# Second input's product moved into the expert rounds, a ring of 22 places, and another route to the first round

## The chip, the cores and the metric

The kernel runs on one core of one Trainium2 chip. The metric is the device time of one execution in microseconds (us), median of three runs. Weights and inputs lie in HBM and come on chip by DMA; TensorE (PE) multiplies into PSUM, VectorE (DVE) and ScalarE (ACT) read PSUM and write SBUF, SyncE (SP) issues nearly all the transfers. Each engine runs its own program in order, and they meet at semaphores.

## The reference

The input is 256 tokens of 1024 features. Two layers of a first block (three attention-like branches and a convolved feed-forward part) are followed by two layers of a second block. The change is in the second block alone, in what follows its attention:

```python
x = layer_norm(ALPHA * x + mix, ln1_g[i], ln1_b[i])
ffn = hierarchical_moe(x, w_route_group[i], b_route_group[i], w_route_expert[i],
                       b_route_expert[i], w_exp_gate[i], w_exp_up[i], w_exp_down[i])
ple = jax.nn.sigmoid(x @ w_ple_gate[i]) * (p[i] @ w_ple[i])
x = layer_norm(ALPHA * x + ffn + ple, ln2_g[i], ln2_b[i])
```

`hierarchical_moe` chooses for each token one of 4 groups and in it the 2 best of 8 experts. There are 32 experts, each with three weight matrices of 1 MiB (gate, up, down). The second input `p` has 256 values a token; `w_ple` is 1 MiB and `w_ple_gate` 4 MiB.

## The kernel before

The second block of a layer runs its attention, then `wo` (four products `out_part(c, k, t)`, half c of the output columns, half k of the rows summed over, tile t of 128 tokens), the first layer norm (`norm_dve_of`, tile by tile on DVE with a square root on ACT), the routing, and then eight **rounds** of four experts each. In a round PE gathers 32 tokens an expert (`gather`, from `xg`, a copy of the normed x that ACT makes in `deal_features`), multiplies by the gate and up chunks (`hidden`, halves 0 and 1), turns, multiplies by the down chunks (`down`) and spreads the rows back (`give`). All 32 experts are always computed, so all 96 MiB of a layer's expert weights come in, and after round steps 1 and 4 the second gate is computed (`second_gate`, 32 matmuls of 512 columns, on 2 chunks of `w_ple_gate`).

**Chunks and the ring.** Every weight chunk of a round is 1 MiB. `expert_chunks` lists them in the order of use; a chunk goes to place j mod 20 of a ring of 20 places (`E_RING`), which lie over tiles that are done by then, and one chunk (`E_ONCE`) to a place that is used once. SP issues the first 21 loads one by one during `wo` and the routing, each as its place comes free (`first_loads(...)` in `sync`). After them `load_again` (L2200) issues each next load when the chunk 20 places earlier has been used. The last four down chunks come in halves (`load_last`, L2211), then the gains of the second layer norm, then the next layer's first chunks into the three `raw` tiles, each after the last expert chunk that lies there (`E_RAW`).

**From `wo` to the first round**, on PE: the eight `out_part`; `second_products(0)`, which is half of p @ w_ple (8 matmuls, L2943); the transposes of tile 0 of the normed x and its routing product (L2955); the same for tile 1; `second_products(1)`; the rank products (L2970 to L2972); the first gather (L2273). DVE computes the choice of experts from the logits (`first_of`, `top_of`; L3205, L3427 to L3461). ACT copies the turned x (`nT`), the two halves of the product (`pl`) and `xg`. `w_ple` has a tile of its own over `dqT`. Each of the last two first loads waits for `pl1`, since they go to `dqT` and to a tile that holds the turned p.

The order on every engine is written out by hand; PSUM halves are handed from user to user in the order of a list (`order`, `expert_lots`).

## Time and profile before

| | us |
|---|---|
| median of 3 runs | 1737.8 |
| lowest and highest | 1737.01, 1740.19 |
| the profiled execution, its own time | 1735.67 |
| its span | 1733.8 |
| PE busy | 1615.5 (93%) |
| DVE busy | 1070.4 (62%) |
| ACT busy | 756.2 (44%) |
| chain that ended last, PE / DMA / DVE | 72% / 12% / 8% |
| bytes moved | 422.82 MB, 244 GB/s in the mean |

The shares are means over stages that have different limits. In the span's slices DMA moves 110 to 200 GB/s for most of the time, and 410 to 418 GB/s in two stretches, about 1065 to 1250 us and 1515 to 1700 us: these are the rounds of the two layers of the second block. The change touches both, and the 80 us ahead of each.

### The profile page before, as it was taken

The page shows a single profiled execution, that of the slowest core. Times are in us where ns is not written, and L with a number is a line of the kernel's source. Part 1 is how long each engine was busy: PE and PEld are TensorE (multiplying, and loading weights), DVE is VectorE, ACT ScalarE, POOL GpSimd, SP SyncE. Part 2 cuts the span into 40 slices and gives each one's busy share as a digit, 9 for nine tenths or more (in the row PEclk, how much of TensorE's full clock was granted, in tenths as well). Part 3 has the DMA queues.
Part 4 walks back from the last instruction along what each step waited for, and adds up shares of the span by engine and source line. Part 5 has one row for each costly group of instructions (what it writes and reads, how often), then busy time and mean ns, then how long its engine had stood idle before and what let it go on. Part 6 is the DMA issues. An engine that isn't in the chain of part 4 may idle for free.

```text
span 1733.8 us, 26050 instructions
## 1 busy us (share of the span) xinstructions
PE 1615.5 (93%) x10632; PEld 1273.2 (73%) x10632; DVE 1070.4 (62%) x1506; ACT 756.2 (44%) x1006; POOL 0.2 (0%) x4
## 2 busy tenths in 40 slices
PE   7999999999999999999999999968779999898775
PEld 7877799998887789999887776534458777654433
DVE  5977768787786858777578762222165887422124
ACT  4556555545546645545455732101034566211111
POOL 0000000000000000000000000000000000000000
PEclk9999999999999999999999999989889999999888
DMA  7543445555553345554656498999965547999996
GB/s 251 175 168 116 164 166 179 189 191 173 189 188 110 127 164 191 187 194 152 210 178 207 147 415 329 416 418 412 411 225 195 201 146 289 362 414 415 413 415 263
DMA packets 174416, 422.82 MB, mean 244 GB/s; under 512 B 16000, under 2 KB 68584, under 8 KB 157672
## 3 DMA queue, kind: packets, MB, share of 16 engines
q1 hardware_dynamic: 174312, 421.33, 66.3%
q8 instruction: 77, 1.26, 0.3%
q14 instruction: 27, 0.22, 0.0%
HBM read 420.25 MB, written 1.05 MB: 243 GB/s over the span
## 4 chain that ended last, share of the span: by engine, by line
PE 72%; DMA 12%; DVE 8%; ACT 3%; SPq 2%; issue 2%; DVEq 0%; ACTq 0%
PE lot L289 18%; PE lot L291 17%; PE lot L290 17%; PE lot L2303 5%; DMA e_lo<-w_exp_up 4%; DMA two_e_sqT<-w_exp_up 3%; DVE w_lo L259 3%; PE lot L2377 2%; PE lot L2273 2%; PE lot L2330 2%; PE lot L416 2%; DMA two_e_dqT<-w_exp_up 2%; DMA two_prq<-w_exp_down 1%; PE lot L485 1%; DMA raw<-w_exp_down 1%
## 5 line engine op out<-in xcount | busy, mean ns | idle before, releaser
L259 DVE TENSOR_TENSOR w_lo<-raw,w_hi 128x2048 fp32r<-128x2048 f32 (+4 forms) x194 | 431.4, 2230 | 103.7 <-ACT w_hi L254 103.0
L254 ACT ACTIVATE w_hi<-raw 128x2048 fp32r<-128x2048 f32 (+4 forms) x194 | 361.2, 1867 | 122.8 <-PE lot L291 116.1
L289 PE MATMUL lot<-one_hT_hi,w_hi 128*128 128x256 f32 x704 | 199.3, 283 | 0.9 <-issue 0.9
L290 PE MATMUL lot<-one_hT_lo,w_hi 128*128 128x256 f32 x704 | 199.2, 283 | 0.0
L291 PE MATMUL lot<-one_hT_hi,w_lo 128*128 128x256 f32 x704 | 199.2, 283 | 0.0
L289 PE MATMUL lot<-w_hi,two_hT_hi 128*128 128x512 f32 (+1 forms) x448 | 176.9, 395 | 6.4 <-DVE two_hT_lo L382 3.1
L291 PE MATMUL lot<-w_hi,two_hT_lo 128*128 128x512 f32 (+1 forms) x448 | 172.5, 385 | 0.0
L290 PE MATMUL lot<-w_lo,two_hT_hi 128*128 128x512 f32 (+1 forms) x448 | 172.3, 385 | 0.0
L289 PE MATMUL lot<-w_hi,one_hT_hi 128*128 128x512 f32 (+2 forms) x384 | 148.7, 387 | 3.0 <-DVE w_lo L259 2.3
L291 PE MATMUL lot<-w_hi,one_hT_lo 128*128 128x512 f32 (+2 forms) x384 | 145.1, 378 | 0.0
L290 PE MATMUL lot<-w_lo,one_hT_hi 128*128 128x512 f32 (+2 forms) x384 | 145.0, 378 | 0.0
L289 PEld LDWEIGHTS lot<-one_hT_hi,w_hi 128*128 128x128 f32 x704 | 135.1, 192 | 2.0 <-issue 1.3
L290 PEld LDWEIGHTS lot<-one_hT_lo,w_hi 128*128 128x128 f32 x704 | 135.1, 192 | 0.7
L291 PEld LDWEIGHTS lot<-one_hT_hi,w_lo 128*128 128x128 f32 x704 | 135.1, 192 | 0.0
L289 PEld LDWEIGHTS lot<-w_hi,two_hT_hi 128*128 128x128 f32 x448 | 85.6, 191 | 26.3 <-issue 8.3
L1803 DVE SCALAR_TENSOR_TENSOR one_conv<-lot,one_cols,one_conv 128x255 f32<-128x255 f32 x160 | 66.2, 476 | 58.2 <-ACT one_conv L1488 55.7
L291 PEld LDWEIGHTS lot<-w_hi,two_hT_lo 128*128 128x128 f32 x448 | 85.5, 191 | 17.0
L290 PEld LDWEIGHTS lot<-w_lo,two_hT_hi 128*128 128x128 f32 x448 | 85.7, 191 | 14.9
L289 PEld LDWEIGHTS lot<-w_hi,one_hT_hi 128*128 128x128 f32 x384 | 72.2, 188 | 20.6 <-DVE w_lo L259 5.5
L291 PEld LDWEIGHTS lot<-w_hi,one_hT_lo 128*128 128x128 f32 x384 | 72.2, 188 | 13.0
L290 PEld LDWEIGHTS lot<-w_lo,one_hT_hi 128*128 128x128 f32 x384 | 72.3, 188 | 11.5
L2428 DVE COPY two_xw<-lot 128x512 f32<-128x512 f32 x16 | 11.1, 692 | 110.9 <-PE lot L2273 110.9
(457 smaller groups left out, 3235.6 us busy)
## 6 DMA issues: line engine op xcount, KB each, us to landing
raw<-w_in SPq DMA_DIRECT2D x78, 1024.0 KB, 5.1
raw<-ffn_w_up SPq DMA_DIRECT2D x44, 1024.0 KB, 5.1
raw<-ffn_w_down SPq DMA_DIRECT2D x22, 1024.0 KB, 5.0
raw<-w_out SPq DMA_DIRECT2D x16, 1024.0 KB, 6.2
e_lo<-w_exp_up SPq DMA_DIRECT2D x12, 1024.0 KB, 19.7
raw<-w_exp_down SPq DMA_DIRECT2D x12, 1024.0 KB, 17.4
e_hi<-w_exp_gate SPq DMA_DIRECT2D x10, 1024.0 KB, 19.1
e_hi<-w_exp_up SPq DMA_DIRECT2D x10, 1024.0 KB, 20.3
```

What stands on the lines that cost most here:

```text
L254: act.activation(K.hi[:, r, 0:n], self.raw(name)[:, 0:n], ACT.Copy).then_inc(K.sig["hi_ready"], 1)
L259: dve.tensor_tensor(K.lo[:, r, 0:n], self.raw(name)[:, 0:n], K.hi[:, r, 0:n].bitcast(F32), ALU.subtract).then_inc(K.sig["lo_ready"], 1)
L289: pe.matmul(out, a[0], b[0], start=start, stop=False)
L290: pe.matmul(out, a[0], b[1], start=False, stop=False)
L291: return pe.matmul(out, a[1], b[0], start=False, stop=stop)
L416: last = pe.matmul(s[:, h, t, 0:n], self.q(u, h)[:, t * P:(t + 1) * P], self.k(u, h)[:, 0:n], start=True, stop=True)
L485: last = pe.matmul(self.K.ps[3][h * HD:(h + 1) * HD, 0, q0:S], self.v(u, h, c), pt[:, h, c, q0:S], start=c == 0, stop=c == T - 1)
L1803: last = dve.scalar_tensor_tensor(dst, src, w, dst, ALU.mult, ALU.add)
L2273: last = pe.matmul(K.ps[1][:, lot - 2, kk * QE * CAP:(kk + 1) * QE * CAP], M.xg[:, t, k, :], M.rows01[:, t, :], start=t == 0, stop=t == T - 1)
L2303: last = pe.matmul(K.ps[0][j * CAP:(j + 1) * CAP, lot, half * D_E:(half + 1) * D_E], M.xw[:, k, rows], w[j][:, k, :], start=k == 0, stop=k ...
L2330: last = pe.matmul(K.ps[2][j * CAP:(j + 1) * CAP, n, :], M.h[:, f, j * CAP:(j + 1) * CAP], w[j][:, f, n * 512:(n + 1) * 512], start=f == 0 ...
L2377: last = pe.matmul(K.ps[1][:, lot - 2, :], M.nT[:, k, t * P:(t + 1) * P], w[:, k % 4, :], start=k == 0, stop=k == KD - 1)
```

## The change

The ring gets 22 places. `yT` and `hT_hi` (the turned x, `nT`) become places, `dqT` and the shared tile move forward in it, and the place used once now takes chunk 18. SP issues 23 loads ahead of the rounds, the last one when the routing product is filled.

The product p @ w_ple leaves the stretch before the rounds. Its weights come as two chunks of 512 KiB (`l0`, `l1`) just ahead of the gate's chunks, and go into a ring place whose other half takes the result. Since `nT` is a ring place now, the second gate turns x again from `xg` in the round (`second_turn`, 16 transposes each time, ACT copies them to the ring place of `n0` or `n1`, for which nothing is loaded); `w_ple_gate` is read in another order of rows to match.

On the way to the first round `out_part(1, 0, 1)` is moved back behind `out_part(1, 1, 0)`, so that tile 0 is complete earlier. The first layer norm gives its two halves of columns one after the other, and the transposes, copies and routing products follow half by half. Transposes of the identity are put between (6, 8, 12 and 4 of them). The choice of experts is rewritten with the top-8 instruction and its replacement over all 32 experts of a token, in place of the chain on 8 values. Some semaphores get other names, which are shared with the first block.

```diff
-E_RING = 20
-E_ONCE = 15
+E_RING = 22
+E_ONCE = 18
 PLE_AT = {0: 1, 1: 4}
 E_LOTS = 7
 LAST_TURNS = 44
-E_RAW = (10, 6, 9)
-E_SPLIT = ((15, 16), (11, 12), (13, 14))
-E_LN2 = 19
+E_RAW = (12, 8, 11)
+E_SPLIT = ((18, 19), (14, 15), (16, 17))
+E_LN2 = 20
+ROUTE_TURNS = (6, 8, 12, 4)
...
-            [K.raw[:, 2, :], K.raw[:, 0, :]] + \
-            [t[:, r, :] for r in (1, 2, 0) for t in (K.plain_hi, K.plain_lo)] + [t[:, :] for t in (e_prv, e_dqT, shared)]
+            [t[:, :] for t in (e_p, e_sqT, e_pt, e_yT, e_dqT)] + [K.raw[:, 1, :]] + \
+            [self.gates[:, t, :] for t in range(T)] + [K.raw[:, 2, :], K.raw[:, 0, :], shared[:, :]] + \
+            [t[:, r, :] for r in (1, 2, 0) for t in (K.plain_hi, K.plain_lo)] + [e_prv[:, :], e_nT[:, :]]
...
-            names += [f"pg{c}{k}" for c in range(2) for k in range(2) if PLE_AT.get(c) == q]
+            for c in range(2):
+                names += [f"n{c}", f"l{c}", f"pg{c}0", f"pg{c}1"] if PLE_AT.get(c) == q else []
...
+        if name[0] != "n":
+            self.wait_out(sp, self.held_before(name))
+            self.load(sp, name, self.expert(name))
...
+    def second_turn(self, pe, c, j):
+
+        name = f"N{c}.{j}"
+        lot = self.claim(pe, name)
+        for k in range(4):
+            last = pe.transpose(self.K.ps[1][:, lot - 2, k * P:(k + 1) * P], self.M.xg[:, j // 2, 4 * (j % 2) + k, :],
+                                self.K.ident[:, :])
+        last.then_inc(self.L.filled(name), 1)
+
+    def second_turned(self, act, c, j):
+
+        if j == 0:
+            self.wait_out(act, self.held_before(f"n{c}"))
+        lot = self.filled(act, f"N{c}.{j}")
+        act.activation(self.features(c)[:, 4 * (j % 2):4 * (j % 2) + 4, (j // 2) * P:(j // 2 + 1) * P],
+                       self.K.ps[1][:, lot - 2, :].rearrange("p (k s) -> p k s", k=4), ACT.Copy)\
+           .then_inc(self.L.drained(f"N{c}.{j}"), 1)
...
+        elif name[0] == "l":
+            eng.wait_ge(self.K.sig["e_placed"], int(name[1]) + 1)
...
+    def second_products(self, pe, c, t):
+
+        K, M = self.K, self.M
+        name = f"L{c}.{t}"
+        lot = self.claim(pe, name)
+        w = self.weights(pe, f"l{c}")
+        for k in range(2):
+            last = pe.matmul(K.ps[1][:, lot - 2, :], M.pT[:, k, t * P:(t + 1) * P], w[:, k, :], start=k == 0, stop=k == 1)
+        last.then_inc(self.L.filled(name), 1)
+
+    def second_taken(self, act, c, t):
+
+        lot = self.filled(act, f"L{c}.{t}")
+        act.activation(self.second(c, t), self.K.ps[1][:, lot - 2, :], ACT.Copy).then_inc(self.L.drained(f"L{c}.{t}"), 1)
+
     def second_gate(self, pe, c, t):
 
         K, M = self.K, self.M
         name = f"P{c}.{t}"
+        if t == 0:
+            for j in range(2 * T):
+                self.drained(pe, f"N{c}.{j}")
...
-            last = pe.matmul(K.ps[1][:, lot - 2, :], M.nT[:, k, t * P:(t + 1) * P], w[:, k % 4, :], start=k == 0,
+            last = pe.matmul(K.ps[1][:, lot - 2, :], self.features(c)[:, k, t * P:(t + 1) * P], w[:, k % 4, :], start=k == 0,
...
+        last.then_inc(self.K.sig["e_placed"], 1)
+        dve.wait_ge(self.K.sig["e_placed"], c + 1)
...
+    x = lambda h: K.x[:, t, h * 512:(h + 1) * 512]
+    centred = lambda h: dve.scalar_tensor_tensor(x(h), x(h), mean, g[:, h * 512:(h + 1) * 512], ALU.subtract, ALU.mult)
+    last = centred(0) if halves else [centred(h) for h in range(2)][-1]
     link(last)
     if between:
         between(dve)
     dve.wait_ge(K.sig[f"{tag}_root"], K.sig.at(f"{tag}_root", t + 1))
     link(dve.reciprocal(inv, K.stat[:, 2 + t:3 + t]))
     for h in range(2):
-        x = K.x[:, t, h * 512:(h + 1) * 512]
-        dve.scalar_tensor_tensor(x, x, inv, b[:, h * 512:(h + 1) * 512], ALU.mult, ALU.add)\
+        if halves and h:
+            link(centred(h))
+        dve.scalar_tensor_tensor(x(h), x(h), inv, b[:, h * 512:(h + 1) * 512], ALU.mult, ALU.add)\
            .then_inc(K.sig[f"{tag}_normed"], 1)
...
-              ("pT", 3), ("nTt0", 0), ("pl0", 3), ("pl1", 2), ("nTt1", 0), ("rt", 1), ("rank", 0), ("count", 0)]
+              ("pT", 3), ("nTt0", 0), ("nTt1", 3), ("rt", 1), ("rank", 0), ("count", 0)]
...
-            return A["w_ple_gate_2"][layer][k * 512:(k + 1) * 512, c * 512:(c + 1) * 512].rearrange("(k p) c -> p k c", p=P)
+            return A["w_ple_gate_2"][layer].rearrange("(p k) c -> p k c", p=P)[:, 4 * k:4 * k + 4, c * 512:(c + 1) * 512]
...
                 first_loads(5)
+                L.wait_filled(sp, "bd1")
+                first_loads(6)
             if name == "wo11":
                 L.wait_filled(sp, "bs1")
-                sp.dma_start(M.w_ple[:, :, :], A["w_ple_2"][layer].rearrange("(k p) c -> p k c", p=P))\
-                  .then_inc(sig["wple_in"], 16)
+                first_loads(7)
         sp.wait_ge(sig["lo_ready"], ST.ready["wo10"])
-        first_loads(6)
+        first_loads(8)
         sp.wait_ge(sig["merged"], sig.at("merged", 4))
-        first_loads(7, 8)
+        first_loads(9, 10)
         sp.wait_ge(sig["lo_ready"], ST.ready["wo01"])
-        first_loads(9)
+        first_loads(11)
         sp.wait_ge(sig["lo_ready"], ST.ready["wo11"])
-        first_loads(10)
+        first_loads(12)
+        L.wait_filled(sp, "pT")
+        first_loads(13)
         ST.wait_used(sp, "wo10")
-        first_loads(11, 12)
+        first_loads(14, 15)
         ST.wait_used(sp, "wo01")
-        first_loads(13, 14)
+        first_loads(16, 17)
         ST.wait_used(sp, "wo11")
-        first_loads(15, 16, 17)
+        first_loads(18, 19, 20)
         sp.wait_ge(sig["n1_normed"], sig.at("n1_normed", 2 * T))
-        first_loads(18)
-        L.wait_filled(sp, "pl1")
-        first_loads(19, 20)
+        first_loads(21)
+        L.wait_filled(sp, "rt")
+        first_loads(22)
...
-        ST.done(out_part(1, 0, 1), "wo10")
         both("mT1")
         out_part(0, 1, 0)
         out_part(1, 1, 0).then_inc(L.filled("wot0"), 1)
+        ST.done(out_part(1, 0, 1), "wo10")
...
+        def turn_normed(t):
+
+            lot = L.claim(pe, f"nTt{t}")
+            dst = flat(K.ps[lot][:, :, :])
+            for k in range(KD):
+                if k % 4 == 0:
+                    pe.wait_ge(sig["n1_normed"], sig.at("n1_normed", 2 * t + k // 4 + 1))
+                last = pe.transpose(dst[:, k * P:(k + 1) * P], K.x[:, t, k * P:(k + 1) * P], K.ident[:, :])
+                if k == 3:
+                    last.then_inc(sig["half_ready"], 1)
+            last.then_inc(L.filled(f"nTt{t}"), 1)
 
         def route_tile(t):
 
@@ -2950,19 +3012,23 @@
             if t == 0:
                 L.claim(pe, "rt")
                 pe.wait_ge(sig["w_route"], sig.at("w_route", 32))
-            both(f"nTt{t}")
+            pe.wait_ge(sig["nT_copied"], sig.at("nT_copied", t + 1))
             for k in range(KD):
+                if k == 4:
+                    both(f"nTt{t}")
                 last = pe.matmul(K.ps[lot][:, t, 0:N_ROUTE], M.nT[:, k, t * P:(t + 1) * P], M.w_route[:, k, :],
                                  start=k == 0, stop=k == KD - 1)
             if t:
                 last.then_inc(L.filled("rt"), 1)
 
-        second_products(0)
-        transpose_tile(K, L, pe, K.x, "nTt0", 0, sig, "n1_normed")
+        turn_normed(0)
+        lot = L.claim(pe, "nTt1")
+        keep_awake(K, pe, lot, ROUTE_TURNS[0])
         route_tile(0)
-        transpose_tile(K, L, pe, K.x, "nTt1", 1, sig, "n1_normed")
+        keep_awake(K, pe, lot, ROUTE_TURNS[1])
+        turn_normed(1)
         route_tile(1)
-        second_products(1)
+        E.warm(pe, ROUTE_TURNS[2])
...
+            lot = L.use[f"nTt{t}"][0]
+            quarter = lambda b: (M.nT[:, 4 * b:4 * b + 4, t * P:(t + 1) * P],
+                                 K.ps[lot][:, b, :].rearrange("p (k s) -> p k s", k=4))
+            act.wait_ge(sig["half_ready"], sig.at("half_ready", t + 1))
+            act.activation(*quarter(0), ACT.Copy).then_inc(sig["nT_copied"], 1)
+            L.wait_filled(act, f"nTt{t}")
+            act.activation(*quarter(1), ACT.Copy).then_inc(L.drained(f"nTt{t}"), 1)
...
-        take("pl1", M.pl[:, 1, :, :], whole)
...
+        link(dve.tensor_reduce(st[:, 140:142], g, AX_X, ALU.max))
+        top = st[:, 140:142].unsqueeze(2).to_broadcast([P, T, N_G])
+        link(tt(small, g, top, ALU.is_equal))
+        tt(M.r[:, 0, :, 0:N_G], g, top, ALU.subtract).then_inc(sig["group_shift"], 1)
+        link(dve.scalar_tensor_tensor(small, small, -100.0, M.iota[:, 0:N_G].unsqueeze(1).to_broadcast([P, T, N_G]),
+                                      ALU.mult, ALU.add))
+        link(dve.tensor_reduce(st[:, 146:148], small, AX_X, ALU.min))
+        link(tt(cold, small, st[:, 146:148].unsqueeze(2).to_broadcast([P, T, N_G]), ALU.is_gt))
+        for t in range(T):
+            last = dve.scalar_tensor_tensor(by_group(M.r32[:, t, :]), cold[:, t, :].unsqueeze(2).to_broadcast([P, N_G, E_G]),
+                                            NEG, by_group(e[:, t, :]), ALU.mult, ALU.add)
+        link(last)
+        for t in range(T):
+            last = dve.max(M.top8[:, t, :], M.r32[:, t, :])
+        link(last)
+        link(dve.memset(M.top8[:, :, 2:8], PICKED))
+        for t in range(T):
+            last = dve.match_replace(M.w32[:, t, :], M.top8[:, t, :], M.r32[:, t, :], PICKED)
+        link(last)
+        dve.tensor_scalar(M.r32_r[:, :, :], M.w32[:, :, :], -2e38, None, ALU.is_lt).then_inc(sig["selected"], 1)
+        tt(M.r32[:, :, :], M.r32[:, :, :], M.top8[:, :, 0:1].to_broadcast([P, T, N_E]), ALU.subtract)\
+            .then_inc(sig["expert_shift"], 1)
```

PE in layer 0 of the second block, from the end of `wo` to the first gather. Before:

```order
L2943 MATMUL lot<-two_w_ple,two_pT 128x512 x4
L886 MATMUL lot<-ident,x 128x128 x8
L2955 MATMUL lot<-two_w_route,two_nT 128x36 x8
L886 MATMUL lot<-ident,x 128x128 x8
L2955 MATMUL lot<-two_w_route,two_nT 128x36 x8
L2943 MATMUL lot<-two_w_ple,two_pT 128x512 x4
L2970 MATMUL lot<-two_r_153,two_tri_r 128x32
L2971 MATMUL lot<-two_r_153,two_tri_r 128x32
L2972 MATMUL lot<-two_r_153,two_tri_r 128x32
L2273 MATMUL lot<-two_rows_143,two_xg 128x128 x16
```

The same place now:

```order
L3004 MATMUL lot<-ident,x 128x128 x8
L894 MATMUL lot<-ident 128x128 x6
L3019 MATMUL lot<-two_w_route,two_nT 128x36 x8
L894 MATMUL lot<-ident 128x128 x8
L3004 MATMUL lot<-ident,x 128x128 x8
L3019 MATMUL lot<-two_w_route,two_nT 128x36 x8
L2402 MATMUL lot<-ident 128x128 x12
L3036 MATMUL lot<-two_r_152,two_tri_r 128x32
L3037 MATMUL lot<-two_r_152,two_tri_r 128x32
L3038 MATMUL lot<-two_r_152,two_tri_r 128x32
L2402 MATMUL lot<-ident 128x128 x4
L2308 MATMUL lot<-two_rows_142,two_xg 128x128 x16
```

Both products on `w_ple` have gone from here (a row's count is that of the instructions written; the trace shows each of these fp32 matmuls as two).

SP in layer 0, from the load of the last `wo` chunk to the eleventh load behind it, before:

```order
L2655 DMA raw<-w_out 128x4x512
L2696 DMA two_w_ple<-w_ple 128x2x1024
L2200 DMA raw<-w_exp_up 128x2048
L2200 DMA two_gates<-w_exp_up 128x2048
L2200 DMA two_gates<-w_exp_gate 128x2048
L2200 DMA raw<-w_exp_gate 128x2048 x2
L2200 DMA e_hi<-w_exp_gate 128x2048
L2200 DMA e_lo<-w_exp_up 128x2048
```

Now, from one load further ahead:

```order
L2211 DMA two_e_yT<-w_exp_up 128x2048
L2713 DMA raw<-w_out 128x4x512
L2211 DMA two_e_dqT<-w_exp_up 128x2048
L2211 DMA raw<-w_exp_gate 128x2048
L2211 DMA two_gates<-w_exp_gate 128x2048 x2
L2211 DMA raw<-w_exp_gate 128x2048
L2211 DMA raw<-w_exp_up 128x2048
L2211 DMA two_e_shared<-w_exp_up 128x2048
```

A load into `yT` stands ahead of the last `wo` chunk, and an expert chunk stands where `w_ple` stood.

PE at the second gate of round step 1, before:

```order
L2273 MATMUL lot<-two_rows_143,two_xg 128x128 x16
L2285 MATMUL lot<-ident,two_wrows 128x128 x2
L2377 MATMUL lot<-two_gates,two_nT 128x512 x16
L2330 MATMUL lot<-raw,two_h 32x512 x2
L2330 MATMUL lot<-e_hi,two_h 32x512
```

Now:

```order
L2308 MATMUL lot<-two_rows_142,two_xg 128x128 x16
L2320 MATMUL lot<-ident,two_wrows 128x128 x2
L2228 MATMUL lot<-ident,two_xg 128x128 x16
L2411 MATMUL lot<-two_e_yT,two_pT 128x512 x4
L2430 MATMUL lot<-two_e_dqT,two_e_pt 128x512 x4
L2430 MATMUL lot<-raw,two_e_pt 128x512 x4
```

The transposes of x and half of p @ w_ple stand ahead of the gate, which now reads its features from a ring place.

## Rows read from the trace of the kernel before

**Rows 1.** Windows, layer 0: stretch, length, engines' busy time, PE clock, DMA share, GB/s.

```profile
1040.00:1045.00 5.00, 3.89 (x18) 3.84 (x18) 0.18 (x1) 4.28 (x3) 0.00 (x0) 0.50 1.03 411
1045.00:1050.00 5.00, 5.00 (x11) 2.06 (x10) 4.24 (x26) 0.59 (x3) 0.00 (x0) 0.73 0.19 78
1050.00:1055.00 5.00, 4.08 (x40) 3.82 (x43) 1.86 (x9) 2.74 (x3) 0.00 (x0) 1.00 0.87 301
1055.00:1060.00 5.00, 5.00 (x88) 2.92 (x84) 1.46 (x5) 0.00 (x0) 0.00 (x0) 1.00 0.46 149
1060.00:1065.00 5.00, 5.00 (x72) 3.76 (x63) 1.54 (x5) 0.76 (x2) 0.00 (x0) 1.00 0.96 403
...
1065.00:1250.00 185.00, 152.18 (x1420) 85.18 (x1419) 44.50 (x76) 23.41 (x35) 0.00 (x0) 0.93 1.02 415
```

**Rows 2.** Windows, layer 1, the same stretch.

```profile
1500.00:1505.00 5.00, 2.81 (x18) 1.96 (x17) 3.82 (x20) 1.02 (x1) 0.00 (x0) 1.00 0.92 329
1505.00:1510.00 5.00, 5.00 (x73) 3.82 (x75) 0.69 (x1) 1.88 (x2) 0.00 (x0) 1.00 0.54 224
1510.00:1515.00 5.00, 5.00 (x87) 2.68 (x76) 1.97 (x7) 0.00 (x0) 0.00 (x0) 1.00 0.62 210
...
1515.00:1700.00 185.00, 155.90 (x1433) 88.32 (x1430) 43.82 (x76) 24.15 (x36) 0.00 (x0) 0.93 1.02 415
```

**Rows 3.** Timeline of SP's queue: start, duration, line, transfer; both layers.

```profile
1049.83 0.37 SPq L2200 DMA_DIRECT2D two_e_dqT<-w_exp_down  x1
1050.24 0.47 SPq L2200 DMA_DIRECT2D two_e_shared<-w_exp_gate  x1
1058.41 0.34 SPq L2200 DMA_DIRECT2D two_e_spare<-w_exp_gate  x1
...
1510.89 0.34 SPq L2200 DMA_DIRECT2D two_e_spare<-w_exp_gate  x1
```

**Rows 4.** Timeline of PE, layer 0, from the end of `wo` to the first gather.

```profile
1030.33 3.59 PE L2943 MATMUL lot<-two_w_ple,two_pT 128*128 128x512 f32 x8
...
1033.76 1.04 PE L886 MATMUL lot<-ident,x 128*128 128x128 f32 x8
...
1044.59 5.20 PE L2943 MATMUL lot<-two_w_ple,two_pT 128*128 128x512 f32 x8
...
1051.00 3.81 PE L2273 MATMUL lot<-two_rows,two_xg 128*128 128x128 f32 x32 [0.92 <-issue]
```

**Rows 5.** Timeline of DVE: layer norm and routing of layer 0, routing of layer 1.

```profile
1036.24 1.42 DVE L2579 SCALAR_TENSOR_TENSOR x<-x,stat,two_ln_b 128x512 f32<-128x512 f32 x2
...
1044.82 0.23 DVE L3205 TENSOR_TENSOR two_logit<-lot,two_route_b 128x72 f32<-128x72 f32 x1 [7.16 <-PE lot L2955]
...
1049.08 0.43 DVE L3205 TENSOR_TENSOR two_r<-two_r 128x16 f32<-128x16 f32 x2
...
1497.31 0.23 DVE L3205 TENSOR_TENSOR two_logit<-lot,two_route_b 128x72 f32<-128x72 f32 x1 [4.31 <-PE lot L2955]
```

**Rows 6.** DVE groups by form: what the top-8 instructions take on 128 values.

```profile
L3287 DVE MAX8 two_top<-two_work 128x8 f32<-128x128 f32 x16 | 4.7, 291 | 0.3
L3291 DVE MATCH_REPLACE8 two_work<-two_top,two_work 128x128 f32<-128x128 f32 x16 | 4.4, 276 | 0.0
```

**Rows 7.** Chain that ended last, rounds of layer 0: start, duration, what.

```profile
1095.45 13.74 PE lot L2377 x32
...
1119.56 25.44 DMA e_lo<-w_exp_up
```

**Rows 8.** End of layer 0: ACT, then DVE, then landing of the next layer's first chunk.

```profile
1267.09 0.68 ACT L254 ACTIVATE w_hi<-raw 128x576 fp32r<-128x576 f32 x1 [0.20 <-DMA raw<-w_in]
...
1272.54 0.16 DVE L2576 RECIPROCAL stat<-stat 128x1 f32<-128x1 f32 x1
...
raw<-w_in SPq DMA_DIRECT2D x1, 288.0 KB, 10.4
...
raw<-w_in SPq DMA_DIRECT2D x1, 288.0 KB, 3.0
```

191 lines of the change are left out of this document (79 added, 112 removed).

## The prediction

> **What bounds the kernel now.** I read the page's slices first, then windows over the rounds, then SP's queue, then PE and DVE between `wo` and the first gather. PE is busy for 93% of the span, but not in the rounds, and the change touches only these and the stretch ahead of them. In the rounds of layer 0 DMA moves 415 GB/s for 185 us on end with a busy share of 1.02, while PE is busy for 152.2 of the 185 us [rows 1]; in layer 1 it is 415 GB/s and 155.9 us [rows 2]. The chain walks there through the landing of a chunk, 25.44 us after its issue [rows 7], so some ten chunks are in flight. The rounds end when their bytes are in. At 415 GB/s a chunk of 1.049 MB costs 2.53 us. The reader should look for the one thing that moves such an end: time in which DMA stands still after it has become full. There is one such hole in each layer. In layer 0 the windows from 1045 to 1065 us show 78, 301, 149 and 403 GB/s [rows 1]. Against 415 that is 20 us less (931/415) x 5 us = 20 - 11.22 = **8.78 us** of lost transfer. In layer 1 three windows show 329, 224 and 210 [rows 2]: 15 - (763/415) x 5 = **5.81 us**.
>
> Why the hole is there: the first 21 loads have been issued, and the next may go only when the first chunk has been used, at 1058.41 us in layer 0 and 1510.89 us in layer 1 [rows 3]. Also the last two first loads went late, at 1049.83 and 1050.24 us [rows 3], since they waited for `pl1`.
>
> **More loads ahead of the rounds.** The total of bytes stays: `w_ple` (1 MiB) leaves the stretch ahead and comes back as two halves, `n0` and `n1` load nothing. Ahead of the first reload stand two loads more and `w_ple` less, so one chunk net, 2.53 us of cover. In layer 0, with about 2 us from the reload's issue to its first bytes (a small transfer of 288 KB landed in 3.0 us on an idle queue [rows 8], of which 0.7 are bytes), the old set was done at 1060.4 - 8.78 = 1051.6 us of transfer time; the new one would be at 1054.2. In layer 1 it is 1512.9 - 5.81 + 2.53 = 1509.6. To leave no hole the first chunk must be used by 1052.2 and 1507.6, which is 6.2 and 3.3 us earlier than now. The new first loads must themselves come in time: counting chunks, the changed list is at every wait level with the old or ahead of it until `wo` is done (`yT` is free early), and the last two, behind the norm and the routing product, are issued by about 1039 us.
>
> **An earlier first gather.** On PE the first eight matmuls of the product take 3.59 us between `wo` and the transposes [rows 4]; they go. DVE finishes the norm of tile 1 at 1036.24 + 1.42 = 1037.66 [rows 5]. With tile 0 filled one `out_part` earlier, DVE is free when tile 1 is filled at about 1030.4. Two operations of half a tile's columns at the rate of L2579 (0.7 us each), the second statistics (0.7), the mean and root (some 0.5) and the centring and scaling (4 x 0.7) put the end at about 1035.6. Transposing 4 of 8 (1.04 us for 8 [rows 4]), a half copy (0.6), and half the routing product (about 1 us) follow, the first halves being done already: logits at about 1038.4 against 1044.82 [rows 5], **6.4 us** earlier. In layer 1, where the clock did not fall, the same steps give 1493.8 against 1497.31 [rows 5], **3.5 us**. The `xg` copies on ACT (2 us each) end before the gather needs them.
>
> **The choice of experts.** From the logits to the end of the selection it is 1049.51 - 1044.82 = 4.69 us now [rows 5]. The new chain has some 14 dependent steps. The top-8 instructions take 291 and 276 ns on 128 values [rows 6]; on 32 I take about 0.2 us, as for the other small DVE operations. The bounds are 0.15 and 0.29 us for each of the four, 0.3 us either way. The sum is about 2.85 us: **1.8 us** less. The second half of the product, 5.20 us of PE beside the old chain [rows 4], is gone too; in layer 0 it ended at 1049.79, no earlier than the selection, so the rank products would otherwise not have profited. Rank, rows and gather keep their 1.5 us. Together the first gather, at 1051.00 now [rows 4], comes 8.2 us earlier in layer 0 and 5.3 us earlier in layer 1. Both are 2.0 us more than is needed. So both holes close: -8.8 and -5.8 us.
>
> **Turns of the identity.** In layer 0 the clock stood at 0.50 of 2.4 GHz from 1040 to 1045 us and was mixed to 1050 [rows 1], after PE had waited for copies; in the same stretch of layer 1 the window shows 1.00 [rows 2]. The 30 transposes fill waits. If they fail, routing product and transposes run at the level of before, 1.2 GHz, and cost up to 2 us more, which is the margin just worked out. Bounds 0 and +2 us; I take 0.
>
> **The second gate in the rounds.** It gains 16 transposes (2.1 us, at 1.04 for 8) and half of the product (3.59 us), with waits for ACT's copies about 7 us in all, beside the 13.74 us that it takes [rows 4, 7], twice in a layer. PE was idle for 32.8 and 29.1 us of each 185 [rows 1, 2], so 14 us fit, and the 10 chunks in flight keep DMA going. Cost 0; uncovered, 14 us a layer. The waits on `e_placed` stand at the end of DVE's step of the gate; behind them are only DVE's adds, on an engine with 44.5 of 185 us busy [rows 1]. The ring place of `n` and the one of `l` are held during a gate of some 21 us, in which 8 chunks land; with `n`, `l` and the two gate chunks held, 18 of the 22 places are left for them.
>
> **Half-size transfers.** The last eight loads of a layer are of 512 KiB already and the stream stays full over them up to 1250 us [rows 1], so the two new ones cost 0 in the sum. The Trainium skill (DMA: Bandwidth & Descriptors, Bandwidth) gives 341 GB/s for a lone 1 MB transfer and 425 for 16 MB and advises at least 1 MiB; halves at, say, 290 GB/s would by that rule add about 0.5 us each, 2 us in all (an estimate from that page). This trace does not agree where the queue is full: 415 GB/s with single chunks of 1 MiB.
>
> **The end of layer 0.** The next layer's first chunk now goes over the place of the last down chunk but two, which is free only when the last matmul is done (about 1266.1 us on the old scale). Before, it landed at 1267.09, 10.4 us after its issue, behind the stream; on an idle queue the like of it took 3.0 us [rows 8]. It would land at about 1269.5. ACT then needs 0.7 + 1.3 + 0.2 + 0.2 us, and its root is wanted by 1272.54 us [rows 8], so it just fits. Bounds: 0 and, with a landing as slow as before, 10.4 - 3.7 = +6.7 us. I take 0, being nearer to the idle row, since nothing else is in the queue.
>
> **Sum.** Against the profiled execution (1735.67 us): -8.8 - 5.8 = -14.6, giving 1721.1. That execution lies 2.1 us under the median of 1737.8; on the median's scale the forecast is **1723.2 us**.
>
> **Rivals.**
> A. *The holes close in part.* The clock falls in the routing all the same, or the half-by-half steps hide less than I count. With 4 us less advance a layer the holes keep 2 us each: -10.6, 1727.2 us. For it: the layers differ by 3 us there now. Against: 2 us of margin in both.
> B. *The hand-over at the end of layer 0 waits for the raw chunk* behind the last matmul, up to +6.7: about 1729.9 us. For it: the sum for ACT is tight. Against: the idle landing.
> C. *The gate starves DMA.* `n`, `l` and two gate chunks are held at once, and DMA pauses for a third of the 14 us of added work, 4.5 us a layer: -14.6 + 9, about 1732 us.
> D. *Nothing moves*, because the stream's rate, not its holes, absorbs the gain (the rate sinks when the first loads come closer): 1737.8 us. Against: full windows on both sides of the hole show the same 415.
> E. *Slower: PE becomes the bound of the rounds.* PE's work in the 185 us of layer 0 becomes 152.2 + 14 = 166 us, of 185 - 8.8 = 176. It is the bound when the granted clock of the rounds falls from 0.93 [rows 1] below 0.93 x 166 / 176 = 0.88, and the gain is lost when PE needs 7.3 us over the 176, at 0.84. At 0.82 it is 188 us, 12 us over, in each layer: 1737.8 - 14.6 + 24 = 1747 us. For it: PE does wait between chunks, and its clock is already mixed. Against: the share of waiting gets smaller.
>
> **How the numbers follow.** Forecast 0.66, A 0.12, B 0.07, C 0.06, D 0.03, E 0.06. The forecast's own range is 1720 to 1726; below it I leave 1718, since timed runs whose clock falls in layer 1 as well have a larger hole (5.8 could be 8.8, 3 us more to gain). Up to 1731 takes in A, B and some of C, so the range is 1718 to 1731, with about 0.15 outside. 0.2% is 3.5 us, about what a measurement of this kernel can tell from no change. Faster by more: forecast, A, B, C, 0.91. Within: D, 0.03. Slower: E, 0.06.
>
> **What would show it.** Right: windows of 5 us show about 415 GB/s with no dip from 1000 us to the end of layer 0's rounds, and in layer 1; 22 loads before the first reload, which is issued near 1050 us; the first gather near 1043 us; the clock at 1.00 in the routing; the gate some 21 us with DMA full. Wrong: a dip that stays, a dip behind the gates, an ACT wait of over 2 us for `raw` at the end of layer 0, or a mean rate in the rounds below 410 GB/s.

## Result and the profile after

Before: 1738.49 us (median of 4 runs, 1737.01 to 1740.19). After: **1724.88 us** (4 runs, 1722.88 to 1727.42). The ratio is 0.9922 with a 95% interval of 0.9905 to 0.994, so 13.6 us less (10 to 17). The forecast was 1723.2 us, with a range of 1718 to 1731. One of the four executions of a kernel below (`halves_p`, 1991.41 us) ran in a slower state, and its ratio leaves that one out.

The profiled execution of after took 1727.42 us (span 1725.6), only 8.2 us less span than the 1733.8 of before. It is the slowest of its four, and the one of before was faster than every timed run beside it, so the two traces have to be compared by stretches. First the transfers: windows of after, layer 0, columns as in [rows 1].

```profile
1035.00:1040.00 5.00, 5.00 (x45) 4.83 (x44) 4.08 (x9) 3.30 (x4) 0.00 (x0) 1.00 1.03 424
1040.00:1045.00 5.00, 4.01 (x35) 3.54 (x33) 2.24 (x12) 4.18 (x4) 0.00 (x0) 1.00 1.01 406
1045.00:1050.00 5.00, 3.59 (x30) 3.38 (x31) 2.98 (x18) 1.25 (x4) 0.00 (x0) 1.00 1.02 408
1050.00:1055.00 5.00, 5.00 (x79) 3.28 (x77) 0.69 (x1) 1.36 (x2) 0.00 (x0) 1.00 1.03 424
1055.00:1060.00 5.00, 5.00 (x77) 3.23 (x77) 2.39 (x8) 0.38 (x1) 0.00 (x0) 1.00 1.01 418
1060.00:1065.00 5.00, 5.00 (x70) 4.02 (x72) 1.09 (x3) 0.60 (x1) 0.00 (x0) 1.00 1.01 421
1065.00:1250.00 185.00, 160.65 (x1458) 91.03 (x1454) 43.54 (x74) 30.36 (x46) 0.00 (x0) 0.95 1.02 413
```

The same in layer 1:

```profile
1495.00:1500.00 5.00, 4.70 (x52) 4.27 (x56) 2.22 (x8) 1.88 (x2) 0.00 (x0) 1.00 1.03 416
1500.00:1505.00 5.00, 5.00 (x90) 2.88 (x85) 1.55 (x7) 0.00 (x0) 0.00 (x0) 1.00 1.02 419
1505.00:1510.00 5.00, 5.00 (x64) 4.08 (x57) 0.90 (x2) 0.98 (x2) 0.00 (x0) 1.00 1.01 423
```

Where [rows 1, 2] had 78, 301, 149 and 329, 224, 210 GB/s, no window is below 406. Both holes are gone, and the clock of the routing in layer 0 is 1.00 (it was 0.50). Why they are gone stands in SP's queue (columns as in [rows 3]): the last two of the first loads, then the first reload, and the same of layer 1.

```profile
1040.68 0.53 SPq L2211 DMA_DIRECT2D two_e_prv<-w_exp_gate  x1
1043.16 0.33 SPq L2211 DMA_DIRECT2D two_e_nT<-w_exp_gate  x1
1054.83 0.33 SPq L2211 DMA_DIRECT2D two_e_spare<-w_exp_gate  x1
...
1491.04 0.33 SPq L2211 DMA_DIRECT2D two_e_nT<-w_exp_gate  x1
1502.71 0.33 SPq L2211 DMA_DIRECT2D two_e_spare<-w_exp_gate  x1
```

And on PE in layer 0, from the end of `wo` over the second tile's routing product and the ranks to the first gather:

```profile
1035.51 1.03 PE L3004 MATMUL lot<-ident,x 128*128 128x128 f32 x8
...
1041.20 1.93 PE L3019 MATMUL lot<-two_w_route,two_nT 128*128 128x36 f32 x16
...
1045.99 0.28 PE L3036 MATMUL lot<-two_r,two_tri_r 128*128 128x32 f32 x1 [1.52 <-DVE two_r L3521]
...
1047.42 3.81 PE L2308 MATMUL lot<-two_rows,two_xg 128*128 128x128 f32 x32 [0.42 <-issue]
```

DVE: the logits and the selection in layer 0, the logits in layer 1.

```profile
1043.17 0.23 DVE L3281 TENSOR_TENSOR two_logit<-lot,two_route_b 128x72 f32<-128x72 f32 x1 [2.52 <-PE lot L3019]
...
1045.74 0.20 DVE L3521 TENSOR_SCALAR two_r<-two_w 128x64 fp32r<-128x64 f32 x1
...
1491.05 0.23 DVE L3281 TENSOR_TENSOR two_logit<-lot,two_route_b 128x72 f32<-128x72 f32 x1 [2.52 <-PE lot L3019]
```

Everything ahead of the rounds lies 5.2 us later in this execution (1035.51 against 1030.33 [rows 4]), so steps are measured from the end of `wo`. The logits come 7.7 us behind it (before 14.5), the first gather 11.9 us (before 20.7), the first reload 19.3 us (before 28.1).

**Where the time went.** The two ends of layer 1's dense part in before are its first product and the end of `wo`:

```profile
1278.68 0.40 PE L289 MATMUL lot<-w_hi,two_hT_hi 128*128 128x72 f32 x1 [3.11 <-DVE two_hT_lo L382]
...
1485.66 3.59 PE L2943 MATMUL lot<-two_w_ple,two_pT 128*128 128x512 f32 x8
```

In after they are 1275.32 and 1483.39 us. That gives four parts:

- from the end of `wo` in layer 0 to layer 1's first product: 248.35 us before, 239.81 after, **-8.5**
- from the end of `wo` in layer 1 to the end: 248.1 before, 242.2 after, **-5.9**
- ahead of layer 0's routing, in code that the change doesn't touch: +5.2
- layer 1's dense part: 207.0 before, 208.1 after, +1.1

The first two sum to -14.4 and are the change. The third is chance: all of it is there by 910 us (the same load of `w_in` is issued at 904.93 us before and at 910.10 after), where both kernels still run the same code. Of its 5.2 us, 3.75 are there by 64 us: a load landed late, and PE's clock fell during the wait. The waits of PE for the first block's latents, before and after:

```profile
PE lot L1127 <- DVE one_lat L1580: 1.3, 1, 1.3
```

```profile
PE lot L1128 <- DVE one_lat L1581: 3.2, 1, 3.2
```

Ten of the kernels traced here share this code and that of the layers ahead, word for word; they issue the load of `two_e_nT` in layer 0 between 1037.73 and 1043.66 us, and after is at 1043.16. That puts the end of `wo` between 1030.1 and 1036.0 us; in the two traces with the old code (before, and `choice` below) it is at 1030.33 and 1032.55. The fourth part comes back below (the hand-over).

### The profile page after: what moved, and what is told of

Read it like the earlier page. It is cut to its first block, busy times and chain, and to the rows that moved or that the text cites. A ratio compares the mean times of both kernels' runs of the same rounds, so it can differ in the third digit from the quotient of the medians.

```text
span 1725.6 us, 26332 instructions
## 1 busy us (share of the span) xinstructions
PE 1623.5 (94%) x10756; PEld 1283.2 (74%) x10756; DVE 1067.8 (62%) x1494; ACT 767.6 (44%) x1030; POOL 0.2 (0%) x4
## 4 chain that ended last, share of the span: by engine, by line
PE 74%; DMA 10%; DVE 9%; ACT 3%; SPq 2%; issue 2%; DVEq 0%; ACTq 0%
PE lot L290 18%; PE lot L292 17%; PE lot L291 17%; PE lot L2338 5%; DMA two_gates<-w_exp_up 4%; DMA two_e_spare<-w_exp_up 3%; DVE w_lo L260 3%; PE lot L2430 3%; DMA two_e_prv<-w_exp_down 3%; PE lot L2308 2%; PE lot L2365 2%; PE lot L417 2%; PE lot L486 1%; ACT w_hi L255 1%; PE lot L476 1%
## 5 line engine op out<-in xcount | busy, mean ns | idle before, releaser
L292 PEld LDWEIGHTS lot<-w_hi,one_hT_lo 128*128 128x128 f32 x384 | 72.6, 189 | 13.1
```

Source lines behind the costliest of these rows:

```text
L292: return pe.matmul(out, a[1], b[0], start=False, stop=stop)
```

## Experiments

All are against the changed kernel, but for the last one. Ratios are to the kernel before on the same chip, whose medians there were 1738.42 (first four), 1739.32 (next four) and 1736.71 us (last four), so kernels of different groups are compared by their ratios: 0.001 is 1.7 us.

**How much earlier than needed the gather is.** Two kernels with turns of the identity ahead of the first gather. A turn is a transpose of the identity whose result nobody reads; it takes PE 0.114 us (44 of them took 5.03).

```diff
         both("rt")
+        E.warm(pe, 35)        # 105 in the second kernel
         E.gather(pe, 0)
```

> The changed kernel with 35 more turns of the identity on PE right ahead of the first gather of each layer: at 0.114 us a turn (44 turns took 5.03 us in the trace of after) 4.0 us of delay, of which about 0.6 us falls into PE's wait for the rows. My theory: after the change the stream has a margin. In the trace of after the last of the first loads is issued at 1043.16 us and lands 17.7 us later, at 1060.9, while the first reload is issued at 1054.83 and needs some 2 us to its first bytes, so about 4 us are to spare in each layer. The delay stays inside it: 1724.9 us, 0 to +1 us. Rival, the gather itself is on the path (PE's work in the rounds is the bound): +3.4 us in each layer, 1731.7 us.

> The same with 105 turns, 12.0 us, of which 11.4 count. My theory: beyond the margin of 4 us every us of delay opens a hole of one us in the transfers, (11.4 - 4) = 7.4 us in each layer, +15 us in all: about 1740 us, and windows of 5 us show the hole near 1060 us as in the kernel before. Rival, the gather on the path from the start: +23 us, 1748 us. Rival, the hole was not what set the time of before: no change, 1725 us.

Measured: 1725.55 us, ratio 0.9923 (0.9899 to 0.9947), and 1739.31 us, ratio 1.0004 (0.9991 to 1.0017). The second has given back the whole gain. Its windows in layer 0 and its first reload:

```profile
1050.00:1055.00 5.00, 5.00 (x48) 5.00 (x47) 0.00 (x0) 0.00 (x0) 0.00 (x0) 1.00 0.61 251
1055.00:1060.00 5.00, 5.00 (x59) 4.45 (x61) 0.69 (x1) 1.88 (x2) 0.00 (x0) 1.00 0.02 7
1060.00:1065.00 5.00, 5.00 (x89) 2.88 (x85) 1.76 (x7) 0.00 (x0) 0.00 (x0) 1.00 0.32 82
```

```profile
1040.02 0.33 SPq L2211 DMA_DIRECT2D two_e_nT<-w_exp_gate  x1
1062.50 0.33 SPq L2211 DMA_DIRECT2D two_e_spare<-w_exp_gate  x1
```

From `two_e_nT` to the first reload it is 11.67 us in after, 14.84 with 35 turns, 22.48 with 105: 3.2 and 10.8 us later. From `two_e_nT` to layer 1's first product it is 232.2, 233.8 and 241.0 us: 1.7 and 8.8 us longer. With 35 turns a small hole is open already (329 and 367 GB/s from 1055 to 1065 us). So the first 1.5 to 2.0 us are free, and from there each us costs about one. By the medians the cost of 105 turns is 14.3 us in two layers, which leaves 3.6 us free in each. The rule holds; how large the margin is stays open between 1.5 and 3.6 us. My 4 us was too large by the traces, and the prediction's 2.0 was nearer.

**Whether ring places and an earlier gather are one sum.** The 35 turns, and two places of cover less:

```diff
         sp.wait_ge(sig["n1_normed"], sig.at("n1_normed", 2 * T))
-        first_loads(21)
         L.wait_filled(sp, "rt")
-        first_loads(22)
+        E.wait_out(sp, E.names[0])
+        first_loads(21)
+        first_loads(22)
```

> The kernel with 35 turns ahead of the first gather, and the last two of the first loads held until the first chunk has been used: the cover of two ring places (5.06 us) is taken away. My theory: the cover and the earlier gather are one sum. The margin of 4 us becomes -1, and the delay of 3.4 us adds to it, so the hole is 3.4 + 5.06 - 4.1 = about 4.4 us in each layer, +8.7 us against the kernel with the turns alone: about 1734 us. If the ring places are worth nothing (only the gather counts), it is as fast as with the turns alone, 1725 us.

Measured: 1735.05 us, ratio 0.998 (0.9968 to 0.9991), 9.5 us over the kernel with the 35 turns alone, where 8.7 were expected. The windows from 1045 to 1060 us are at 360, 29 and 360 GB/s. Two places less are worth what 5 us of later gather are.

**The turns in the routing.**

```diff
-ROUTE_TURNS = (6, 8, 12, 4)
+ROUTE_TURNS = (0, 0, 0, 0)
```

> The changed kernel without the 30 turns of the identity in the routing. My theory: the granted clock falls to 0.50 in the routing of layer 0 as it did before the change, the gather comes up to 2 us later there, and the margin of 4 us takes that: 1724.9 us, 0 to +1. Rival, the turns are what makes the change work: the gather comes 4 us or more later in both layers and the hole comes back in part, +2 to +6 us, 1727 to 1731 us.

Measured: 1726.18 us, ratio 0.9929 (0.9905 to 0.9952). One window of layer 0, and one of layer 1:

```profile
1040.00:1045.00 5.00, 1.30 (x5) 1.22 (x6) 3.71 (x24) 1.59 (x3) 0.00 (x0) 0.50 1.02 409
```

```profile
1500.00:1505.00 5.00, 5.00 (x92) 2.90 (x84) 1.42 (x7) 0.00 (x0) 0.00 (x0) 1.00 0.69 234
```

The clock falls to 0.50 again, and now in layer 1 too (0.50 from 1485 to 1495 us, where before and after both show 1.00). The transfers do not stay full: 393 and 390 GB/s from 1050 to 1060 us, and the 234 shown in layer 1. From the end of `wo` the first reload takes 22.2 and 23.8 us, where after has 19.3 in both layers: 2.9 and 4.5 us more. The stretches behind the end of `wo` (to layer 1's first product, and to the end) take 241.1 and 244.7 us against 239.8 and 242.2: 1.3 and 2.5 us more. That is once more the delay less 1.5 to 2.0 us. The traces so put the price of leaving the turns out at 3.8 us, the medians at 1.3 (ratio +0.0007), which is within the spread. My expectation that the margin takes the delay is not what the windows show; they show the rival's picture, a hole that comes back in part, while the time is not told apart from no change.

**Room for PE in the rounds.** 5 and 15 us more ahead of each gate.

```diff
+                    E.warm(pe, 44)        # 132 in the second kernel
                     E.second_gate(pe, c, 0)
```

> The changed kernel with 44 more turns of the identity on PE (5.0 us) ahead of each of the two gates of a layer, 20 us of PE work in all. My theory: PE has room in the rounds (160.65 us busy of the 185 us from 1065 to 1250 in the trace of after), the gate grows from about 20 to 25 us, ten loads cover it, and the time stays: 1724.9 us, 0 to +1. Rival, the gate already stands at the edge of starving the transfers or PE is the bound: +5 us a gate, up to +20 us, 1745 us.

> The same with 132 turns, 15 us a gate, 60 us of PE work in all. My theory: now PE is the bound of the rounds: 160.65 + 30 = 190.7 us of work in 185 us, so at least +6 us a layer, +12 us, about 1737 us; up to +25 us if transfers stop while a gate of 35 us holds four chunks and uses none. Windows of 5 us then show dips of the transfers behind the gates. Rival, no limit near: 1725 us. Rival, each gate is on the path: +60 us, 1785 us.

Measured: 1724.99 us, ratio 0.9927 (0.9903 to 0.995), and 1744.87 us, ratio 1.0033 (1.0015 to 1.0051). 5 us a gate are free; with 15 it is 19 to 20 us slower than the changed kernel. Windows of layer 0 with 132 turns, the gate from 1091 to 1125 us:

```profile
1115.00:1120.00 5.00, 5.00 (x13) 2.21 (x12) 0.69 (x1) 0.58 (x1) 0.00 (x0) 1.00 1.04 420
1120.00:1125.00 5.00, 5.00 (x13) 2.09 (x11) 0.00 (x0) 0.00 (x0) 0.00 (x0) 1.00 0.59 247
1125.00:1130.00 5.00, 5.00 (x57) 1.85 (x60) 0.69 (x1) 1.48 (x2) 0.00 (x0) 1.00 0.59 210
1130.00:1135.00 5.00, 4.68 (x58) 2.61 (x46) 4.34 (x7) 1.80 (x3) 0.00 (x0) 1.00 0.31 75
```

SP issues no load from 1105.5 to 1125.4 us in this trace, and the transfers run dry some 17 us into that. This is rival C's mechanism, at a gate of 34 us; at 20 us (after) and 25 us (44 turns) it does not appear. PE's busy time is 176.06 of the 185 us from 1065 to 1250, so my first estimate, that PE's sum of work would be the bound there, is not what this shows: the dip comes first.

**What a transfer in halves costs.** Every reload but the last ones as two transfers, split along the rows.

```diff
-        sp.dma_start(self.chunk(name), self.source(name[0], expert)).then_inc(self.landed(name), 16)
+            for n in range(2):
+                sp.dma_start(dst[:, n * KD // 2:(n + 1) * KD // 2, :], src[:, n * KD // 2:(n + 1) * KD // 2, :])\
+                  .then_inc(self.landed(name), 16)        # down chunks: by halves of the columns
```

> The changed kernel with every reload of 1 MiB in the rounds but the last ones split into two transfers of 512 KiB, on the same queue one behind the other; some 37 chunks a layer. My theory: behind a full queue the size of a transfer from 1 MiB down to 512 KiB costs nothing: 1724.9 us, -1 to +1, with 413 GB/s in the rounds. Rival, the size rules the rate even in a full queue, at the half microsecond for each MiB in halves that the prediction named: 37 x 0.54 = 20 us a layer, 1765 us.

Measured: 1737.98 us, ratio 0.9999 (0.9986 to 1.0012): 13 us slower than whole transfers, so my theory fell. The count of 37 was wrong as well: SP issues 152 transfers in layer 0's rounds instead of 83, so 69 are split in a layer, and 13.1 / 138 is **0.10 us for each MiB**, not 0.54. The queue from 1065 to 1240 us, after and with halves (a gate or up chunk comes in packets of 8 KB, and with halves only 12 of 26488 packets are that long, where after has 5116 of 14940):

```profile
DMA packets 14940, 72.41 MB, mean 414 GB/s; under 512 B 1120, under 2 KB 1120, under 8 KB 9824
```

```profile
DMA packets 26488, 69.80 MB, mean 399 GB/s; under 512 B 2058, under 2 KB 2058, under 8 KB 26476
```

By the sources in the code, a gate or up chunk of a partition is one contiguous piece of 8 KB, a down chunk two of 4 KB, a chunk of the gate's weights four of 2 KB; halves are 4 KB and 2 KB. The rates of the windows follow: some 420 GB/s for 8 KB, 405 to 410 for 4 KB, 386 to 397 for 2 KB, and with halves they alternate between 410 and 388. Two kernels test whether it is the piece or the transfer that counts.

```diff
+            for n in range(2):
+                sp.dma_start(dst[n * 64:(n + 1) * 64], src[n * 64:(n + 1) * 64]).then_inc(self.landed(name), 16)
```

> The changed kernel with the same reloads split in two as before, but by partitions: 64 and 64, so that no contiguous piece gets shorter, while each transfer is again of 512 KiB. Splitting along the rows cost 13 us and took the rate in the rounds from 414 to 399 GB/s, with 26488 packets instead of 14940 in 175 us. Theory A, the length of the pieces set that: 1724.9 us, -1 to +1, and 414 GB/s. Theory B, the size of the transfer or the number of transfers set it: about 1738 us again.

Measured: 1923.56 us, ratio 1.1047 (1.1015 to 1.1078). Neither theory has this: transfers to 64 partitions have a price of their own, much larger than the one sought (281 GB/s, below). The Trainium skill (DMA: Bandwidth & Descriptors, Rules for kernel authors) advises against two transfers to disjoint halves of the partitions, since they serialize. This trace agrees with the advice, and it shows more than serializing would cost: 281 GB/s where whole transfers, one behind the other, had 415. This run doesn't separate A from B. The next one does, with transfers of the same size and longer pieces:

```diff
-        return rows.rearrange("(k p) c -> p k c", p=P) if kind == "D" else rows.rearrange("(p k) c -> p k c", p=P)
+        return rows.rearrange("(p k) c -> p k c", p=P)
...
-            last = pe.transpose(K.ps[3][:, 0, f * P:(f + 1) * P], M.act[:, 1, f * P:(f + 1) * P], K.ident[:, :])
+            last = pe.transpose(K.ps[3][:, 0, f * P:(f + 1) * P], M.act[:, 1, :].rearrange("s (p f) -> s f p", f=2)[:, f, :],
+                                K.ident[:, :])
```

> The kernel with both groups of hand-over turns, and in it w_exp_down read so that each partition's two rows lie side by side in memory (pieces of 8 KB instead of 4 KB; PE's transpose of the activations picks every second column to match). In the trace of after the windows of the rounds show about 420 GB/s where gate and up chunks are loaded (pieces of 8 KB) and 388 to 410 where down chunks are. My theory: the length of the piece sets the rate. 24 down chunks of 1 MiB a layer at about 403 GB/s take 2.60 us, at 420 GB/s 2.50: 2.4 us a layer, -5 us against the kernel with the turns alone, about 1714 us. Rival, the dips have another cause (loads beside ACT's and DVE's work, or the order on the queue): no change.

Measured: 1720.08 us, ratio 0.9893 (0.9873 to 0.9912), 3.6 us under the kernel it is built on (`hand2` below, 1723.69; 0.9898 to 0.9936), where 5 were expected. The two intervals overlap, so the gain in time is likely rather than certain; in the two traces the stretches behind the end of `wo` are 0.6 us (layer 0) and 2.6 us (layer 1) shorter. The rates are clearer. The window from 1090 to 1240 us of after, with halves, with longer pieces, and by halves of the partitions:

```profile
1090.00:1240.00 150.00, 127.35 (x1059) 69.58 (x1062) 36.10 (x62) 26.08 (x39) 0.00 (x0) 0.94 1.02 415
```

```profile
1090.00:1240.00 150.00, 123.65 (x1017) 65.93 (x1015) 34.10 (x58) 23.19 (x34) 0.00 (x0) 0.92 1.04 400
```

```profile
1090.00:1240.00 150.00, 129.77 (x1072) 71.11 (x1074) 36.08 (x62) 26.20 (x39) 0.00 (x0) 0.94 1.02 419
```

```profile
1090.00:1240.00 150.00, 92.58 (x694) 49.68 (x693) 23.06 (x41) 16.48 (x26) 0.00 (x0) 0.81 1.02 281
```

(`hand2` has 415 GB/s there, as after has.) With longer pieces most of the dips go to 415 to 424 GB/s, and what is left at 1070 to 1080, 1165 to 1175 and 1245 to 1255 us (385 to 406) are, by the order of the loads, the chunks of the gate's weights and the last halves, both of 2 KB pieces. So the piece sets the rate (together with the distance in memory between the pieces of a partition, which changes with it). Whether the number of transfers adds something was not separated; whole chunks of 4 KB pieces and halves of 4 KB pieces both ran at 405 to 410.

**The hand-over between the layers.** In after PE waits 5.27 us for DVE's norm behind the last product, then 2.64 us for the first operand. The clock, 0.82 from 1265 us, is at 0.50 from 1270, and it stays there until about 1285.2 us (the window from 1285 shows 0.98):

```profile
1280.00:1285.00 5.00, 5.00 (x18) 4.42 (x19) 1.23 (x1) 2.57 (x2) 0.00 (x0) 0.50 0.61 204
```

Two kernels:

```diff
         E.give_half(pe, NQ - 1, 1)
+        if before is None:
+            E.warm(pe, 40)                        # the first kernel asks `if out is None`, see below
...
         if ahead:
             keep_awake(K, pe, lot, INDEX_TURNS)
+        if before:
+            keep_awake(K, pe, lot, 18)
```

> The changed kernel with 40 turns of the identity behind the last product of layer 0 and 18 more between the transposes of the next layer's first tile and its first product. In the trace of after PE is idle for 5.3 and 2.6 us there, the granted clock falls to 0.50 until about 1285.2 us, and 9.9 us of work at half the clock cost 4.9 us, the eight transposes 0.9 more. My theory: with the turns the clock stays at 1.00 over the hand-over: -4 to -6 us against the changed kernel, about 1720 us. Rival, the clock falls all the same, or the turns stand in front of the transposes: 0 to +1 us, 1725 us.

> The kernel with the turns at the hand-over from layer 0 to layer 1, now with both groups: 40 turns behind the last product of layer 0 (the run before this one held only the 18 behind the transposes of the first tile, since a name in the code meant something else there; it came to 1719.4 us, and its granted clock rose at about 1270.6 us instead of 1285.2). My theory: with both the clock does not fall at all, the eight transposes of the first tile take 1.04 us instead of 1.94, and that is on the path: 0.9 us less, 1718.5 us. Rival, the 18 turns have all there is to gain: 1719.4 us.

In the first the condition on the 40 turns read a name that PE's part of the code uses for something else, so only the 18 turns ran. Measured: **1719.44 us, ratio 0.9895** (0.9876 to 0.9915), and with both groups 1723.69 us, ratio 0.9917 (0.9898 to 0.9936). The 18 turns alone take 5.4 us off the changed kernel (4.7 by the ratios), as expected of both groups; the 40 give 3.8 to 4.3 us of it back. PE with 18 turns:

```profile
1266.99 1.94 PE L887 MATMUL lot<-ident,x 128*128 128x128 f32 x8 [5.25 <-DVE x L2634]
1268.72 3.07 PE L894 MATMUL lot<-ident 128*128 128x128 f32 x18
1271.54 0.28 PE L290 MATMUL lot<-w_hi,two_hT_hi 128*128 128x72 f32 x1
```

And with both groups:

```profile
1265.77 4.53 PE L2402 MATMUL lot<-ident 128*128 128x128 f32 x40
1275.08 1.93 PE L887 MATMUL lot<-ident,x 128*128 128x128 f32 x8 [4.78 <-issue]
```

With 18 turns the products of layer 1 start at 0.28 us each (0.40 in after): the clock is back after the turns, some 4 us behind the end of PE's wait, not 14. With both groups the clock did not stay up as expected: the eight transposes take 1.93 us again. With the 40 turns PE waits 4.78 us and the profile shows no engine that it waits for. Behind these turns stands the conditional jump over the overflow rounds. In after the same 4.8 us could lie inside the wait for DVE, and the turns, queued ahead of the jump, would push it out from under that cover. That the jump is the cause is read from the place and the releaser "issue", and no run moves the jump alone.

The clock also accounts for the +1.1 us of the fourth part: PE is busy at half the clock for 9.9 us behind the hand-over in after (1275.3 to 1285.2), for 7.9 in before (1278.7 to 1286.6, with the window from 1285 at 0.84). 2 us more at half the clock cost 1.0 us. That the change is the reason is not shown. In seven more traces with the same code at this place the time at half the clock, counted up to the first 512-column product at full speed, runs from 7.6 us (no turns in the routing) and 8.2 (35 turns) to 9.8; by this count after has 9.9, and the two traces with the old code 8.1 each.

**The new choice of experts alone**, in the kernel before (DVE's chain from the logits to the weights as in the change, all else as before; the diff is that part of the change).

> The kernel before with one part of the change alone, the new choice of experts. The selection gets 1.9 us shorter (from the logits to the first gather 6.18 us before, 4.25 after, in layer 0). My theory: in layer 0 the second half of PE's product (at half the clock) ends at 1049.79 us, where the old selection ended at 1049.51, so the gather comes no earlier and the hole stays; in layer 1 the product ends at about 1500.8 us, and the hole there shrinks by 1.9 us: 1738.4 - 1.9 = 1736.5 us. Rival, both layers gain: 1734.6 us. Rival, the selection is not on the way to the first reload: 1738.4 us.

Measured: 1737.12 us, ratio 1.0002 (0.9989 to 1.0015). The interval of 4.5 us holds the -1.9 of the theory barely and rules the rival's -3.8 out. PE in layer 0 of this kernel:

```profile
1046.43 5.62 PE L2943 MATMUL lot<-two_w_ple,two_pT 128*128 128x512 f32 x8
1051.48 0.58 PE L2970 MATMUL lot<-two_r,two_tri_r 128*128 128x32 f32 x1
```

The ranks wait for nothing but PE's own product, as expected, and the windows from 1045 to 1065 us (275, 102, 318, 228 GB/s) hold a hole of 8.9 us, as before. In layer 1 it is (1245 - 876) / 415 x 5 = 4.4 us instead of 5.8. So no gain in time is shown for the selection alone, and in layer 0 the trace shows none in the hole. That it pays once the product has left its place is argued from these rows; no run has the rest of the change without it.

## Why the prediction was right, step by step

**The bound.** Transfers bound the rounds, and the holes were the only loss. Right: the change took -8.5 and -5.9 us where -8.8 and -5.8 were forecast, and opening a hole again by delay alone gave the whole gain back, at one us for one us.

**More loads ahead.** One chunk of net cover is 2.53 us. The run with two places less confirms the trade: 9.5 us for two layers, 8.7 by this sum. The sign of 22 loads ahead of the first reload was miscounted: SP issues 23 (numbers 0 to 22), as the change says, and the trace has the first reload as the 24th.

**An earlier gather.** Forecast 6.4 us for the logits in layer 0 and 3.5 in layer 1; measured from the end of `wo` 6.8 and 4.0 (in layer 1 11.65 to 7.66 us). First gather: forecast 8.2 and 5.3 earlier; measured 8.8 and 5.9. The half us is an addition in the prediction. From the norm's end at 1035.6 us its steps (0.5, 0.6 and 1) give logits at 1037.7, and it wrote 1038.4. On its scale the trace has the norm's end at 1035.5 and the logits at 1038.0. The margin of 2.0 us is 1.5 to 2.0 in the traces, 3.6 by the medians.

**The choice of experts.** Forecast 1.8 us; from the logits to the gather it is 6.18 us before and 4.25 after, 1.9. MAX8 and MATCH_REPLACE8 on 32 values took 0.29 us (two together, pipelined) and 0.17, inside the bounds.

**Turns of the identity.** Forecast 0 with a bound of +2. They did not fail: the clock is 1.00. But the price named for their failure was low. Without them the first reload comes 2.9 and 4.5 us later and the clock falls in layer 1 too, so the margin does not cover it: +3.8 us by the traces, +1.3 by the medians, inside the spread.

**The second gate.** Forecast a gate of about 21 us and no cost. It runs from 1091.7 to 1111.8 us, and nothing stops. The chain through it and behind:

```profile
1094.44 3.66 PE lot L2411 x8
1098.10 13.73 PE lot L2430 x32
...
1120.85 20.87 DMA two_gates<-w_exp_up
```

Behind the gate the chain is a landing again, as in [rows 7].

**Half-size transfers.** The step put them at 0 from windows that read 415 GB/s. This is the step with a wrong term, small only because the change has two of them a layer: the pieces get shorter, and the rate with them. Measured is 0.10 us for each MiB that is cut, so about 0.1 us a layer for the two loads, which are one MiB together. The mean over 185 us hid it; one full window of 5 us in [rows 1], from 1040 us, already lay at 411 beside it. The Trainium skill's rule that the prediction set against the row (DMA: Bandwidth & Descriptors, Bandwidth) points the right way. Its figures are for lone transfers that GpSimd issues. The estimate from them was also added up wrongly: from 341 to 290 GB/s is 0.54 us for each MiB, so 0.27 for each half and 1.1 us in all, where the prediction wrote 0.5 for each half and 2. Half a us for each MiB is still five times what this full queue shows.

**The end of layer 0.** Forecast a landing some 3 us after its issue and ACT just in time. ACT's first piece, DVE's reciprocal, PE's first product:

```profile
1265.99 0.68 ACT L255 ACTIVATE w_hi<-raw 128x576 fp32r<-128x576 f32 x1 [2.58 <-DMA raw<-w_in]
```

```profile
1269.06 0.17 DVE L2630 RECIPROCAL stat<-stat 128x1 f32<-128x1 f32 x1
```

```profile
1275.32 0.40 PE L290 MATMUL lot<-w_hi,two_hT_hi 128*128 128x72 f32 x1 [2.64 <-DVE two_hT_lo L383]
```

The upper bound of +6.7 us took off 3.7 that no row gives; from the prediction's own times it is 1266.1 + 10.4 + 2.4 - 1272.54 = 6.4. The prediction named an ACT wait of over 2 us for `raw` as a sign against it, and the wait is 2.58. But ACT's root is done at 1268.3 and is wanted at 1269.06: the wait falls into time that nobody needs. The sign was badly chosen; a wait of DVE for the root would have been the right one. What this place cost in the trace was elsewhere: the clock came back 2 us later, 1.0 us, which no step had. It is about the difference between the -14.6 of the sum and the -13.6 of the medians, but the return of the clock differs by as much between traces (7.6 to 9.9 us), so this match may be chance.

**Rivals.** A needed holes that stay; none did. B's wait was covered. C exists, but at a gate of 34 us, not 20. D is out. E is out: the clock of the rounds was 0.95 in layer 0 and 0.94 in layer 1, and PE had 24 and 23 us to spare of 185.
